# One normalisation pass moved from VectorE to ScalarE for half of the blocks, and a weight load given its own signal

## The reference

```python
def rmsnorm(x, w):
    xf = x.astype(jnp.float32)
    r = xf * lax.rsqrt(jnp.mean(xf * xf, axis=-1, keepdims=True) + EPS)
    return (r * w.astype(jnp.float32)).astype(x.dtype)
...
        mix = jnp.concatenate([y_ssd.astype(h.dtype), y_hg.astype(h.dtype)], axis=-1)
        h = h + mix @ w_out[l]
        h = h + peer_ffn(rmsnorm(h, ln_ffn_w[l]), w_query[l], sub_keys[l], u_table[l], v_table[l])
    return rmsnorm(h, ln_final_w)
```

## Time and profile before

| what | value |
|---|---|
| median of 3 runs | 3568.52 us (3566.56 to 3569.66) |
| the profiled execution | 3566.36 us |
| its span in the trace | 3564.6 us |
| TensorE busy | 3433.9 us, 96% of the span |
| VectorE busy | 2685.6 us, 75% |
| ScalarE busy | 1081.4 us, 30% |
| GpSimd busy | 1416.9 us, 40% |
| mean granted clock of TensorE | 0.987 of full |

### The profile page before, as it was taken

How to read it: one execution, slowest core, us unless ns; L and a number is a source line. 1 busy time by engine, 2 the same in 40 slices (tenths; PEclk the granted TensorE clock), 3 DMA queues, 4 the chain that set the end, 5 groups by cost and what they waited for, 6 DMA issues and landing times.

```text
span 3564.6 us, 39196 instructions
## 1 busy us (share of the span) xinstructions
PE 3433.9 (96%) x11593; PEld 1966.6 (55%) x11593; DVE 2685.6 (75%) x6453; ACT 1081.4 (30%) x2723; POOL 1416.9 (40%) x1232
## 2 busy tenths in 40 slices
PE   7999999999998999788899999999999999999998
PEld 4666666777775666565344444444444444444443
DVE  2466685566664478797888888887888888888898
ACT  3233344444443222286112121211221212121213
POOL 1000000000001477301656666665565566655665
PEclk9999999999999999899999999999999999999999
DMA  3111003000113343267999999999999999999998
GB/s 113 30 36 36 0 24 115 28 25 24 30 42 143 95 88 66 45 177 251 399 393 378 379 391 386 385 377 356 394 373 383 383 399 378 379 393 386 376 392 334
DMA packets 316334, 836.34 MB, mean 235 GB/s; under 512 B 41696, under 2 KB 147296, under 8 KB 307040
## 3 DMA queue, kind: packets, MB, share of 16 engines
q0 software_dynamic: 165888, 537.01, 40.4%
q1 hardware_dynamic: 127472, 233.75, 18.3%
q10 hardware_dynamic: 22768, 63.18, 4.6%
HBM read 796.03 MB, written 37.81 MB: 234 GB/s over the span
## 4 chain that ended last, share of the span: by engine, by line
PE 50%; issue 4%; DVE 2%; DMA 1%; POOL 0%; ACT 0%; ACTq 0%; DVEq 0%; POOLq 0%
PE peer_ps_o L2075 24%; PE peer_ps_d L2062 22%; PE peer_ps_q L1992 3%; DMA peer_vr<-in_v_rows,peer_index 1%; DVE peer_mt L2260 0%; DVE peer_mt L2264 0%; DMA peer_ur<-in_u_rows,peer_index 0%; PE peer_ps_s L2007 0%; DVE Y L2300 0%; POOL peer_vr L1967 0%; POOL peer_ur L1960 0%; PE peer_ps_o L2043 0%; DVE peer_ur L2289 0%; DVE peer_chosen L1285 0%; DVE route_apart L1281 0%
## 5 line engine op out<-in xcount | busy, mean ns | idle before, releaser
L1960 POOL DMA_INDIRECT peer_ur<-in_u_rows,peer_index x512 | 576.8, 1127 | 588.7 <-DVE peer_ur L2289 419.0
L2300 DVE SCALAR_TENSOR_TENSOR Y<-peer_vr,osq,Y 128x1024 f32<-128x1024 f32 x512 | 656.4, 1282 | 101.3 <-DMA peer_vr<-in_v_rows,peer_index 101.0
L1967 POOL DMA_INDIRECT peer_vr<-in_v_rows,peer_index x512 | 574.6, 1122 | 330.3 <-issue 143.0
L2289 DVE SCALAR_TENSOR_TENSOR peer_ur<-peer_ur,Y 128x1024 f32<-128x1024 f32 x512 | 627.9, 1227 | 6.3 <-DMA peer_ur<-in_u_rows,peer_index 6.3
L2062 PE MATMUL peer_ps_d<-hnT,route_ut 128*128 128x512 f32 x1376 | 598.6, 592 | 0.7 <-ACT peer_vr L2135 0.7
L2075 PE MATMUL peer_ps_o<-hw,Y 128*128 128x512 f32 x1024 | 447.6, 597 | 12.5 <-DVE Y L2276 12.5
L2075 PE MATMUL peer_ps_o<-hnT,Y 128*128 128x512 f32 x1024 | 442.6, 592 | 0.0
L2062 PEld LDWEIGHTS peer_ps_d<-hnT,route_ut 128*128 128x128 f32 x1376 | 261.2, 190 | 328.6 <-issue 327.7
L2075 PEld LDWEIGHTS peer_ps_o<-hw,Y 128*128 128x128 f32 x1024 | 195.5, 191 | 255.9 <-issue 237.5
L2075 PEld LDWEIGHTS peer_ps_o<-hnT,Y 128*128 128x128 f32 x1024 | 193.5, 190 | 238.2 <-issue 238.2
L2062 PE MATMUL peer_ps_d<-hnT,peer_ut 128*128 128x512 f32 x672 | 296.7, 595 | 6.4 <-ACT Y L2143 6.4
(11 more groups left out here) (334 smaller groups left out, 4860.8 us busy)
## 6 DMA issues: line engine op xcount, KB each, us to landing
route_ut<-in_u_cols SPq DMA_DIRECT2D x86, 512.0 KB, 7.5
hw<-in_v_cols SPq DMA_DIRECT2D x16, 2048.0 KB, 10.4
peer_mt<-sel ACTq DMA_DIRECT2D x64, 512.0 KB, 7.9
hnT<-in_v_cols SPq DMA_DIRECT2D x16, 2048.0 KB, 13.6
peer_ut<-in_u_cols SPq DMA_DIRECT2D x42, 512.0 KB, 7.4
route_wk<-in_w_route ACTq DMA_DIRECT2D x14, 1024.0 KB, 7.5
route_wk<-in_w_route SPq DMA_DIRECT2D x10, 1024.0 KB, 4.7
w_group<-in_w_ssd SPq DMA_DIRECT2D x16, 512.0 KB, 4.1
```

Of the source, the lines that this page charges most:

```text
L1960: pool.indirect_dma_start(ur[:, r % RING, :], None, u_rows, bass.IndirectOffsetOnAxis(ap=index[:, r // TOPK % 4, r % TOPK:r % TOPK + 1], a ...
L1967: pool.indirect_dma_start(vr[:, r % RING, :], None, v_rows, bass.IndirectOffsetOnAxis(ap=index[:, r // TOPK % 4, r % TOPK:r % TOPK + 1], a ...
L2289: nc.vector.scalar_tensor_tensor(out=ur[:, s, :], in0=ur[:, s, :], scalar=1.0, in1=Y[:, b, D:MIX], op0=ALU.mult, op1=ALU.mult, accum_out=d ...
L2300: nc.vector.scalar_tensor_tensor(out=hb, in0=vr[:, s, :], scalar=hid[:, c:c + 1], in1=hb, op0=ALU.mult, op1=ALU.add).then_inc(comb_done, 1)
```

## The change

For blocks 0 to 3 VectorE's part of the norm ends with the reciprocal. The product with `rs` is a ScalarE instruction of its own (`normal`), and the weights are put on where ScalarE copies the transposed rows out of PSUM: there a channel is a partition, so that the weights are a scale by partition, from a small array `fk` (128 by 8), and a part is copied with four instructions instead of one. Blocks 4 to 7 keep VectorE's product with `fw`. `fk` is loaded behind `mw` and takes the second place in `s_in`; `fw` has a signal of its own, `fw_in`, for which VectorE waits at block 4.

```diff
         mw = sb("mw", [P, MT])
+        fk = sb("fk", [P, KT])
...
             sp.dma_start(mw[:], mix_w).then_inc(s_in, 16)
+            sp.dma_start(fk[:], ffn_k).then_inc(s_in, 16)
             load_x(0)
             load_w(3)
-            sp.dma_start(fw, ffn_w).then_inc(s_in, 16)
+            sp.dma_start(fw, ffn_w).then_inc(fw_in, 16)
             load_x(1)
...
             def x_copy(b, part):
                 act.wait_ge(x_turned, 2 * b + part + 1)
                 to = xnT[:, 0, :, cols(b)] if b < DB else R.xg[:, :, cols(b - DB)]
-                nc.scalar.activation(to[:, part * 4:(part + 1) * 4, :], ps_x[:], ACT.Copy).then_inc(x_out, 1)
+                if b >= DB:
+                    nc.scalar.activation(to[:, part * 4:(part + 1) * 4, :], ps_x[:], ACT.Copy).then_inc(x_out, 1)
+                    return
+                for j in range(4):
+                    k = part * 4 + j
+                    ins = nc.scalar.activation(to[:, k, :], ps_x[:, j, :], ACT.Copy, scale=fk[:, k:k + 1])
+                ins.then_inc(x_out, 1)
+
+            def normal(b):
+                act.wait_ge(h_inverse, past(b + 1))
+                nc.scalar.activation(Y[:, b, D:MIX], Y[:, b, 0:D], ACT.Copy,
+                                     scale=rs[:, b:b + 1]).then_inc(xn_ready, 1)
...
             nc.scalar.activation(osq[:, HC:NB, :], osq[:, HC:NB, :], ACT.Sqrt).then_inc(rooted, 1)
+            normal(0)
             x_copy(0, 0)
...
                 if b == FIRST:
+                    normal(b - 1)
                     x_copy(b - 1, 0)
                     x_copy(b - 1, 1)
...
                 if 1 <= b <= DB:
+                    normal(b - 1)
                     x_copy(b - 1, 0)
...
             def norm_h(b):
                 dve.wait_ge(h_rooted, past(b + 1))
                 nc.vector.reciprocal(rs[:, b:b + 1], rs[:, b:b + 1]).then_inc(h_inverse, 1)
+                if b < DB:
+                    return
+                if b == DB:
+                    dve.wait_ge(fw_in, 16)
                 dve.wait_ge(h_inverse, past(b + 1))
                 nc.vector.scalar_tensor_tensor(out=Y[:, b, D:MIX], in0=Y[:, b, 0:D], scalar=rs[:, b:b + 1], in1=fw,
                                                op0=ALU.mult, op1=ALU.mult).then_inc(xn_ready, 1)
...
             mean_h(0)
-            dve.wait_ge(s_in, 32)
             norm_h(0)
```

More of the change, by code:

```diff
@@ L1328, in now, with mix_out @@
         self.hold()
-def mix_out(nc, x, w_out, mix_w, ffn_w, w_route, sel, sel_zeroed, hw, hold, C, Y, osq, xnT, R):
+def mix_out(nc, x, w_out, mix_w, ffn_w, ffn_k, w_route, sel, sel_zeroed, hw, hold, C, Y, osq, xnT, R):
     with ExitStack() as ctx:
@@ L1392, in w_row @@
             return w[:, k - FIRST_K, :]
-        w_in, s_in, x_in = [plain_sem(f"w_in{g}") for g in range(NG)], plain_sem("s_in"), [plain_sem("x_in0"), plain_sem("x_in1")]
+        w_in, s_in, fw_in, x_in = [plain_sem(f"w_in{g}") for g in range(NG)], plain_sem("s_in"), plain_sem("fw_in"), [plain_sem("x_in0"), plain_sem("x_in1")]
         meaned, rooted, inverse = sem("meaned"), sem("rooted"), sem("inverse")
@@ L2369, in _, with block_program @@
                 norm(f)
-def block_program(nc, x, ln_w, w_ssd, par, w_hg, lb_logits, w_out, mix_w, ffn_w, w_route, u_cols, v_cols, u_rows, v_rows,
+def block_program(nc, x, ln_w, w_ssd, par, w_hg, lb_logits, w_out, mix_w, ffn_w, ffn_k, w_route, u_cols, v_cols, u_rows, v_rows,
                   fin_w, sel, out):
@@ L2392, in block_program @@
         R = Route(nc, ctx, osq[:, 0:DB, :].rearrange("p b h -> p (b h)"), hw)
-        mix_out(nc, x, w_out, mix_w, ffn_w, w_route, sel, sel_zeroed, hw, hold, C, Y, osq, hnT, R)
+        mix_out(nc, x, w_out, mix_w, ffn_w, ffn_k, w_route, sel, sel_zeroed, hw, hold, C, Y, osq, hnT, R)
         late.close()
@@ L2430, in laid_out @@
         "ffn_w": np.broadcast_to(first("ln_ffn_w"), (P, D)),
+        "ffn_k": first("ln_ffn_w").reshape(KT, P).T,
         "w_route": np.concatenate([first("w_query").reshape(KT, P, PH, 2 * P).transpose(2, 1, 0, 3).reshape(PH, P, -1),
```

## The result

Over 20 runs each, the changed kernel took a median of 3574.33 us against 3567.74 for the kernel before; the ratio is 1.0017, with a 95% interval of 1.0010 to 1.0024, so 3.6 to 8.6 us slower, 6.1 in the middle. The prediction had +3.2, and +6.6 as the upper bound of its sum. The middle is inside the 0.2% (7.1 us) that I called no change, the interval reaches a little beyond it and is clear of one.

A forecast was written before the change was run, and what follows sets the result against it. TensorE's queue was taken to bound the kernel. Start -9.6, copies +1.5, block 2 +2.4, block 3 +6.0 and clock +2.9 gave +3.2 on 3568.52: 3571.7 us, eight in ten 3562 to 3578.

The forecast's parts named there:

- The kernel's end moves with TensorE's queue in this stage, one to one.: Whatever shifts TensorE's queue in the changed stage shifts the end of the kernel by the same amount.
- The start, -8.8: Start of stage: ScalarE no longer waits for the wide weights, so TensorE's first products begin at 1143.1 instead of 1151.93.
- The clock there: First sixteen records: the half clock might not come at the new start; another -0.8, making -9.6 (bounds -10.6 and -8.8).
- Copies in four, +1.5: Copies of blocks 0 and 1: four pieces take 0.55 us more; +1.0 at block 1, +0.5 before it (bounds +1.0, +2.2).
- `normal` of block 2, +2.4: Block 2's transposes wait for ScalarE's product ahead of the copy, starting at 1243.6 instead of 1241.15.
- Of block 3, +6.0: Block 3's transposes wait for ScalarE's gate and product in the turn of block 4: 1300.6 against 1294.64.
- The clock after the stops, +2.9: Slow clock behind TensorE's stops: +1.2 at block 2 (0 to +2.4), +1.7 at block 3 (+0.7 to +2.4).
- What the profile after would show: Forecast trace: first `out_y` near 1142.6, products near 1143.1, second set 1150.6 to 1152.4, two stops, shifted VectorE additions.
- Work taken from VectorE is worth nothing: Four VectorE passes of 1.29 us saved gain nothing further: VectorE waits for blocks 0 and 1; 2 and 3 already counted.
- the slower one: Rival: full clock cost at start, block 1's copy gaps and both stops; sum +8.3, 3576.8 us; chance 0.13.
- The faster rival: Rival: start pays, stops do not come; -8.1, 3560.4 us, or about -2.7 with block 3's stop halved; chance 0.11.
- The other two: Rivals: `fk` lands with the large transfers, +12.8 at most (0.04); ScalarE's product takes 3.9 us, +8.8 (0.02).

The follow-up runs named there:

- the start filled: Kernel before with wide weights on their own signal, plus three unread 128 by 256 products between first transposes and first products: ratio 0.9960, repeated 0.9970.
- filler: Changed kernel with unread TensorE products in its two stops, 2 before block 2's rows and 6 before block 3's: 3568.70 us, ratio 1.0003 to the kernel before.
- product_vector: Changed kernel with the product back on VectorE, by the reciprocal alone, weights still put on by the copies in four: 3560.81 us, ratio 0.9982 to before.
- product_early: Changed kernel with ScalarE's product of blocks 2 and 3 moved to the turn before, behind the third query's copy: 3560.45 us, ratio 0.9981 to before.
- block3_early: Changed kernel with ScalarE's product of block 3 alone in the turn before, block 2's left in place: 3565.06 us, ratio 0.9993 to before.
- the signal alone: Kernel before with the wide weights on their own signal, ScalarE waiting only for the small ones: 3558.40 us, ratio 0.9973; repeated 0.9976.
- the filled kernels: Kernels with unread products in TensorE's pauses: at the stage's start (0.9960, 0.9970), also before block 4's second transposes (0.9966), or in the changed kernel's stops (1.0003).
- late_signal: Changed kernel with ScalarE's queue again waiting for the wide weights at its first wait, as before: 3583.00 us, ratio 1.0044 to the kernel before.

## Why the prediction was right, and where its sizes were off

The direction and the places were as predicted: slower by a little, from an early start and two stops behind ScalarE's product. The size was not: 6.1 us by the ratio and 5.9 by the stage where I had 3.2, near the upper bound of my sum. The waits came out to a few tenths of a us; what I had too low was the clock. By its own steps:

- *The kernel's end moves with TensorE's queue in this stage, one to one.* Right: in twelve profiles with stages from -13.8 to +14.3 us the total by the ratio stays within 2 us of the stage, but for the first measurement of the start filled (3.4). I had read the page's last nineteen slices as nine tenths or more; the last one is an 8, and it changes nothing.
- *The start, -8.8.* Right: -9.1, and the landing of `fk` after 1.9 us. *The clock there*, for which I took another -0.8: wrong in sign in this profile. The first records took 0.6 us longer than before, so that the step as a whole is -8.5 and not -9.6. Against 6.9 us at the full clock they lost 3.0, which is 6 us at half the rate; before they lost 2.4. One profile does not settle this term. The same queue, with `fk`, is at the start of four more kernels: there the first records took 9.85 and 9.84 us (filler, product_vector) and 8.66 and 8.67 (product_early, block3_early; for the latter two the second set is 9.7 and 9.6 earlier, as I had forecast). But in these last two the query behind block 1's gaps then ran slow, 8.83 us instead of 7.14. At the products behind that query the gain was 6.8 us in the three kernels of the first kind and 6.3 in the two of the second, and not the 8.1 of my -9.6 and +1.5: the time won at one place was paid at the other.
- *Copies in four, +1.5.* Right in size: +1.6. The two gaps at block 1 have 1.1 of it, as forecast. The other 0.5 came by another way than mine: not through `out_y` and its banks, but because block 0's second transposes wait for the copy of its first part (0.36 us idle at 1163.85, where the kernel before went on). The experiments give 2 to 3 by the ratios and 4 to 4.5 by the stage, in which slow stretches are included.
- *`normal` of block 2, +2.4*: +2.41. *Of block 3, +6.0*: +5.91, with the gate ahead of it at 1298.53 against 1299.58, 0.7 us earlier once TensorE's own shift at that place (0.3) is taken off, as forecast. The product takes 1.14 us where I took 1.1 (from the row of the square, which has no scale by partition), and the transposes start 0.05 behind its end, where I took 0.1 that no row had shown. The Trainium skill, "ScalarE: Activation LUTs", section "What ACT_TABLE_LOAD costs", gives 186 ns and 0.833 ns for each column, and 93 for an operand by partition: an estimated 1.13 for 1024 columns, and the trace agrees.
- *The clock after the stops, +2.9*: +1.74 and +2.25, together 4.0. The term was mis-sized by 1.1, half of it at each stop: I had 1.2 for block 2, half of what the slow stretch at the start cost, and it came with 1.7; I had 1.7 for block 3, and it came with 2.3. The filler shows that it is the clock, and its size.
- The sum was +3.2; the stage gives +5.9, made of +1.1 at the start, +1.1 for the clock, +0.1 for the copies, and 0.5 between the last product and the last stage. Of that 0.5, 0.3 stands inside VectorE's last routing, between its instructions of L1275 and L1277 (0.72 us apart instead of 0.36). It is there in all five profiles in which ScalarE makes the rows of blocks 0 to 3, and in none of the others; why is open. Both large misses are on one resource: I valued pauses by their waiting and gave the clock the benefit of the doubt twice.
- *What the profile after would show*, less the 2.39 us ahead of the stage: the first `out_y` at 1142.4 and the first products at 1142.9, each 0.2 ahead of the forecast; the second set at 1152.8, 0.4 beyond my range. VectorE's additions of blocks 1 to 4 moved by -8.5, -6.8, -2.7 and +4.4 us, where I had -8 to -9 twice, -4 and +3: from block 2 on each is late by 1.2 us or more.
- *Work taken from VectorE is worth nothing*: right, from both sides. With the product on VectorE or early on ScalarE the time is the same.

Of the rivals, the slower one (every stop costs the clock in full, +8.3, chance 0.13) deserved more. It named four places, and at three of them it came: the start was no faster than before, and both stops brought nearly a full slow stretch. Its own sum without the fourth place, -8.8 + 1.5 + 2.4 + 6.0 + 4.8, is +5.9, which is the stage (to a tenth by luck: its slow stretches at the stops are 0.8 too high, its start is 0.3 too low, and the 0.5 at the end is in none of its terms). The fourth, the query behind block 1's gaps, ran at full clock in the changed kernel's profile and in two others, and slow in three with the same gaps. The forecast was right in its verdict because 6 us still are under 0.2%; its margin was 1 us. The faster rival was wrong in the way expected: nothing gave the stops back. The other two are out as well: `fk` landed after 1.9 us, and the product took 1.14.

## What to carry to other kernels

An instruction moved to an engine with time to spare is priced by where it stands in that engine's queue: list what is ahead of it and which of these wait, and who waits for its result at that moment. Here two instructions cost 13 us or nothing that could be seen, by their place. And look at what a wait counts: the gain of this change was one semaphore shared by an 8 KB and a 512 KB transfer, at the head of a queue that needed the small one; taken alone it is worth 9 us, and the rest of the change more than took it back.

## What the runs showed of the hardware that I had not expected

- Short pauses cost the clock as well. With the signal alone TensorE was idle for 1.85 us ahead of its first transposes of the stage, did these in 1.06, and was idle for another 1.25. The products began at the full clock and fell to half within half a us (0.54 in the window from 1143 to 1144). With 1.3 us of products in the second gap, and the first one left as it was, the clock stayed at 1.00. The Trainium skill, "TensorE: Matmul & The Clock Gate", section "Part 1: The HAM clock gate", says that the lower level is the default and that activity lifts it. With activity holding off the lower level the filled kernels agree; that the lower level is the default no run here shows.
- Which pause brings the half clock is not fixed by its length. The gaps of 1.23 and 1.32 us at block 1's copies left a query of 7.14 us in three profiles (changed kernel, filler, product_vector) and one of 8.83 in three (product_early, block3_early, late_signal). The first records of the stage took 8.66 or 8.67 us in four profiles and 9.84 to 9.90 in three, all behind pauses of 1.23 to 1.61 us; behind 10.6 and 10.96 us they took 9.29 and 9.19. The stop of 2.25 us at block 2 left 8.22 us in the changed kernel and 8.72 with block 3's product early (from the transposes to the products behind the query it is 9.96 in both, 1.7 over the kernel before); and behind the same stop of 2.25 us the old wait's kernel shows no slow stretch:

```profile
1247.85 0.66 PE L1485 MATMUL mo_ps_x<-ident,Y 128*128 128x128 f32 x4 [2.25 <-ACT Y L1600]
...
1249.22 7.07 PE L1506 MATMUL hold<-hnT 128*128 128x256 f32 x32
```

- ScalarE's copy with a scale by partition takes 380 ns for 128 columns and 1140 for 1024; VectorE's product of 1024 columns takes 1286 ns with two tensors and 844 with one and a scale.
